# Weights of a 32-expert layer: 4 MB transfers in the second ring round and in the last expert but one

## What is computed

```python
logits = xf @ w_router + b_router
top_v, top_e = lax.top_k(logits, TOP_K)            # 4 of 32 experts a row
gates = jax.nn.softmax(top_v, axis=-1)
...
def run_block(args):                               # the rows of one expert
    e, toks, g = args
    xb = xf[toks]
    h = xb @ w1[e] + b1[e]                         # w1[e]: 1024 x 2048 float32, 8 MB
    glu = jnp.minimum(h[:, ::2], SWIGLU_LIMIT)
    lin = jnp.clip(h[:, 1::2], -SWIGLU_LIMIT, SWIGLU_LIMIT)
    a = glu * jax.nn.sigmoid(SWIGLU_ALPHA * glu) * (lin + 1)
    out = a @ w2[e] + b2[e]                        # w2[e]: 1024 x 1024 float32, 4 MB
    return out * g[:, None]
...
y = x2 + jax.nn.sigmoid(x2 @ w_ple_gate) * (p @ w_ple)
```

## Time and profile before

| | |
|---|---|
| median of 3 timed runs | 1106.73 us (1106.31 to 1110.37) |
| the profiled execution | 1111.12 us |
| its span, first to last instruction | 1109.3 us |
| TensorE busy | 1082.3 us, 98% of the span |
| VectorE, ScalarE, GpSimd busy | 40%, 14%, 7% |
| moved by transfers | 440.69 MB, 397 GB/s over the span |
| mean granted TensorE clock | 0.993 of full speed |

### The profile page before, as it was taken

The page is one execution under the profiler, slowest core; times in us unless marked ns, Lnnn a source line. Parts: engine busy times, 40 slices in busy tenths (PEclk is TensorE's granted clock), DMA queues, the critical chain, the costliest instruction groups (busy, mean ns, idle before and its releaser), DMA issues.

```text
span 1109.3 us, 14786 instructions
## 1 busy us (share of the span) xinstructions
PE 1082.3 (98%) x5608; PEld 426.0 (38%) x5608; DVE 438.5 (40%) x1109; ACT 159.6 (14%) x306; POOL 78.9 (7%) x107
## 2 busy tenths in 40 slices
PE   9999999999999999999999999999999999999998
PEld 7786423333333333333333333333333333333334
DVE  1648663333333333333333333333333333333345
ACT  1532331110000000000000000000000000000033
POOL 0747411000000000000000000000000000000000
PEclk9999979999999999999999999999999999999999
DMA  9989979999999999999999999999999999999961
GB/s 316 267 313 399 265 310 392 414 425 422 434 432 434 431 429 431 431 432 435 434 428 430 434 430 435 435 427 431 432 429 433 434 426 432 432 426 426 428 256 40
DMA packets 41027, 440.69 MB, mean 397 GB/s; under 512 B 8816, under 2 KB 16236, under 8 KB 25653
## 3 DMA queue, kind: packets, MB, share of 16 engines
q1 hardware_dynamic: 39945, 439.00, 95.0%
q0 software_dynamic: 368, 0.57, 0.3%
q10 hardware_dynamic: 676, 0.59, 0.2%
HBM read 436.61 MB, written 3.77 MB: 397 GB/s over the span
## 4 chain that ended last, share of the span: by engine, by line
PE 67%; DMA 20%; DVE 9%; issue 2%; POOL 1%; ACT 1%; DVEq 0%; SPq 0%; POOLq 0%; ACTq 0%
PE bank L1014 28%; DMA ring<-in_w_mlp 19%; PE bank L1092 16%; PE bank L961 5%; PE bank L605 3%; DVE proj L1651 3%; PE bank L1172 3%; PE bank L784 3%; DVE proj L1648 2%; DVE proj L1646 2%; PE bank L1073 1%; PE bank L974 1%; PE bank L1009 1%; POOL ring L2128 1%; PE bank L967 1%
## 5 line engine op out<-in xcount | busy, mean ns | idle before, releaser
L1014 PE MATMUL bank<-ring,proj 128*64 128x512 f32 x2024 | 463.2, 599 | 7.9 <-DMA ring<-in_w_mlp 7.9
L1612 DVE SCALAR_TENSOR_TENSOR xT<-bank,proj,xT 128x512 f32<-128x512 f32 x128 | 90.2, 746 | 431.2 <-PE bank L961 429.9
L1014 PEld LDWEIGHTS bank<-ring,proj 128*64 128x64 f32 x2024 | 137.7, 137 | 289.3 <-issue 263.6
L1092 PE MATMUL bank<-ring,pool_side 128*64 128x512 f32 x1024 | 226.8, 595 | 0.4 <-ACT pool_side L1981 0.4
L1092 PEld LDWEIGHTS bank<-ring,pool_side 128*64 128x64 f32 x1024 | 71.7, 137 | 133.3 <-issue 130.4
L1975 ACT ACTIVATE proj<-proj 128x256 f32<-128x256 f32 x64 | 26.7, 417 | 518.9 <-DVE proj L1645 518.9
L1603 DVE TENSOR_SCALAR proj<-bank,ln_rows_of_fours 128x64 f32<-128x64 f32 x256 | 67.4, 335 | 24.8 <-PE bank L974 24.8
L961 PE MATMUL bank<-mixT 64*128 64x512 f32 x264 | 74.5, 641 | 0.5 <-ACT mixT L1984 0.5
L605 PE MATMUL bank<-xT,ring 128*128 128x264 f32 x320 | 74.3, 388 | 0.3 <-ACT proj L1797 0.3
L605 PEld LDWEIGHTS bank<-xT,ring 128*128 128x128 f32 x320 | 60.0, 190 | 12.3 <-issue 1.6
L940 PE MATMUL bank<-xreg,proj 128*64 128x512 f32 x248 | 58.5, 592 | 0.0
(11 more groups left out here) (369 smaller groups left out, 638.5 us busy)
## 6 DMA issues: line engine op xcount, KB each, us to landing
ring<-in_w_mlp SPq DMA_DIRECT2D x77, 4096.0 KB, 27.2
ring<-in_w_mlp SPq DMA_DIRECT2D x36, 2048.0 KB, 12.1
ring<-in_w_in SPq DMA_DIRECT2D x9, 1024.0 KB, 15.2
ring<-in_w_out SPq DMA_DIRECT2D x4, 1024.0 KB, 9.0
ring<-in_w_ple_gate SPq DMA_DIRECT2D x4, 1024.0 KB, 28.5
xreg<-in_x_prompt SPq DMA_DIRECT2D x4, 512.0 KB, 4.1
ring<-q_row SPq DMA_DIRECT2D x1, 2048.0 KB, 7.3
ring<-k_row SPq DMA_DIRECT2D x1, 2048.0 KB, 7.2
```

The lines of the kernel that those rows point to most:

```text
L1014: last = pe.matmul(first_bank(t, q), xgT[:, k % 4, k // 4, :], first_columns(rows_, t, q), start=False, stop=(k == KD - 1))
L1092: last = pe.matmul(bank[4][BLOCK * h:BLOCK * (h + 1), :], aT[:, m, BLOCK * t:BLOCK * (t + 1)], w[:, k % 2, 512 * h:512 * h + 512], start=F ...
L1612: ins = STT(total[:, c, s], ins_bank[h][:, :], gate_table[:, c, bass.ds(n, 1)], total[:, c, s], ALU.mult, ALU.add)
```

## The change

The second and third ring round of the first body are loaded by a new function `load_quad` as eight transfers of 4 MB, each waiting for four used units, in place of sixteen of 2 MB, each waiting for two. In the last body only expert 31 is still loaded by pairs; expert 30 now comes as three 4 MB transfers in place of six pairs. `landed` follows: TensorE waits before every fourth unit there, and the counts that it waits for are adapted. `load_late(1)` stays behind the last transfer of the first body.

```diff
@@ -51,7 +51,7 @@
 SLOT = 2048
 UNITS = 12
 FIRST = 4
-LAST_PAIRS = (2, 3)
+LAST_PAIRS = (3,)
 COLUMNS_IN = (0, 512, 1024, 1536, 2048)
 T_U, T_Q, T_K, T_V, T_O = range(0, 20, 4)
 TILES = 20
@@ -447,6 +447,10 @@
                 sp.dma_start(pair_place(s), pair_weights(e, u)).then_inc(sem(f"slot{s}"), 16)
 
 
+            def load_quad(e, n):
+
+                sp.dma_start(quad_place(slot_of(n)), quad_weights(e, n % UNITS)).then_inc(sem(f"slot{slot_of(n)}"), 16)
+
             def load_next(n):
 
                 load_pair(n // UNITS, n // UNITS, n % UNITS)
@@ -487,10 +491,10 @@
             load_next(6)
             sp.wait_ge(sem("mix_ps"), 5)
             load_next(14)
-            for n in range(SLOTS, UNITS * STEP, 2):
-                sp.wait_ge(sem("units_used"), n - SLOTS + 2)
-                load_next(n)
-                if n == SLOTS + 30:
+            for n in range(SLOTS, UNITS * STEP, 4):
+                sp.wait_ge(sem("units_used"), n - SLOTS + 4)
+                load_quad(n // UNITS, n)
+                if n == SLOTS + 28:
                     sp.wait_ge(sem("ple_ps"), 3)
                     load_late(1)
 
@@ -508,7 +512,7 @@
                             load_pair(e + j, j, v)
                     else:
                         sp.wait_ge(sem("units_used"), done + (n - SLOTS + 4))
-                        sp.dma_start(quad_place(slot_of(n)), quad_weights(e + j, u)).then_inc(sem(f"slot{slot_of(n)}"), 16)
+                        load_quad(e + j, n)
 
             bodies = EXPERTS // STEP
             last = (bodies - 1) * STEP
@@ -977,12 +981,12 @@
             def landed(u, i4, closing, opening):
 
                 s = slot_of(u)
-                if opening:
+                if opening and u < SLOTS:
                     if u % 2 == 0:
                         pe.wait_ge(sem(f"slot{s}"), 16 * (before[s] + landings(u)))
                 elif closing == 2 and u // UNITS in LAST_PAIRS:
                     if u % 4 == 2:
-                        seen = STEP * UNITS // SLOTS + sum(slot_of(v) == s for v in range(UNITS * LAST_PAIRS[0], u + 1))
+                        seen = 1 + sum(slot_of(v) == s for v in range(UNITS * LAST_PAIRS[0], u + 1))
                         pe.wait_ge(sem(f"slot{s}"), 16 * (before[s] + seen))
                     elif u % 4 == 0:
                         pe.wait_ge(sem(f"slot{s}"), i4 * 12 + 16 * (before[s] + landings(u) - (s == slot_of(0))))
```

## The result

| | before | after |
|---|---|---|
| median of the timed runs | 1108.43 us (7 runs, 1106.31 to 1110.37) | 1112.93 us (7 runs, 1110.71 to 1115.61) |
| profiled execution, its span | 1111.12, 1109.3 us | 1114.90, 1113.1 us |
| mean granted TensorE clock of the profiled execution | 0.993 | 0.994 |

The ratio is 1.0043, with a 95% interval of 1.0027 to 1.0058: +4.5 us in the medians, +3.8 us between the two profiled spans. It is slower, by less than the 0.5% that counted as a difference. The forecast was +3.7 us.

The account below looks back on a forecast made before the run. The prediction took the weight queue, never resting from 244 us at 431 GB/s, to bound the kernel. Front +2.5 and expert 30 +1.2 gave +3.7 us on 1106.73, so 1110.4 us, range 1105.5 to 1115 us.

Parts of the forecast that it names:

- What bounds the kernel: From 244 us the weight queue runs at 431 GB/s without pause; time it loses earlier is lost at the end.
- The front step: Second ring round in 4 MB transfers: queue stays empty 5.7 us longer, first body transfer ends later, +2.5 us.
- The start-up: Second ring round: the empty queue begins, in effect, 1.4 us after its first issue, at 164.45.
- The bytes by 254 us: Queue from 157 to 254 us: 37.7 MB moved, before 38.7; more than 38.2 would refute the front step.
- The gaps: Among the eight 4 MB transfers: queue idle 1.1 us before the issue at 183.65, 0.9 before 213.74.
- The first wait: TensorE's first wait for weights comes one or two experts before 607 us.
- The lower bound of 0.9: Front step with no start-up at all: sixth issue still holds the end back to 255.1, at least +0.9 us.
- "hidden" rival: Front loss hidden: start-up next to nothing, no wait at expert 30; +0.9, 1107.6 us; chance 0.14.
- The end step: Expert 30: TensorE waits for whole 4 MB transfers, two waits of about half a microsecond; +1.2 us.
- Larger transfers save a fixed cost: Rival: each of eleven transfers fewer saves 2.2 us; -24 us, 1082 us; chance 0.06.
- 4 MB transfers flow worse beside the opening round's work: Rival: the eight transfers flow at 399 GB/s; +4.2 more, +7.9 in all, 1114.6 us; chance 0.16.
- The sum: Whole kernel: front 2.5 plus end 1.2 make +3.7 us, 1110.4 us, +0.33%; chance 0.64.

Follow-up runs that it names:

- e1: Changed kernel with 4 MB transfers in ring rounds two and three only, experts 30 and 31 in pairs: 1111.53 us, ratio 1.0027 to before.
- e3: Kernel before with the 2 MB transfers of rounds two and three issued by twos after four used units: 1111.58 us, ratio 1.0029 to before.
- e6: e1 with two 4 MB transfers issued together behind each wait for eight used units: 1120.99 us, ratio 1.0114 to before.
- e9: Kernel before with no pairs at the end, experts 30 and 31 both in 4 MB transfers: 1110.30 us, ratio 1.0025 to before.
- e2: Kernel before with only expert 30 in three 4 MB transfers, first body still in pairs: 1108.28 us, ratio 0.9998 to before.
- e5: Kernel before with all expert weights in 2 MB pairs, each behind a wait for two used units: 1112.96 us, ratio 1.0041 to before.
- e7: Kernel before with the first 4 MB transfer of the second body (expert 4) split into two pairs: 1108.28 us, ratio 0.9996 to before.

## Why the prediction was right

*What bounds the kernel* held: the steady rate stayed at 431 and 432 GB/s, waits for weights grew from 7.9 to 11.1 us, and a loss ahead of 244 us reached the end with nothing regained that the runs can show, in two sizes: 3.0 and 3.2 us where 2.5 was forecast (e1, e3), 12.6 where 12.2 was (e6).

*The front step*, +2.5 us: e1 measured 3.0 (1.4 to 4.5), and the trace of the change has 2.8, or 3.1 from its earlier issues. The start-up was as forecast: 374 x 7 = 2.62 MB by 170 us are 6.1 us at 431, so the queue began at 163.9, 1.2 us after its issue. The bytes by 254 us were forecast as 37.7 MB and were 37.5, so the first transfer of the body ended at 254 + (38.80 - 37.54) / 0.431 = 256.9 instead of the 256.5 forecast. The gaps are only in part where the forecast put them: against 431 GB/s the queue lost 1.1 us from 170 to 183 us (396), where none was forecast, 1.6 from 183 to 214 (409), where 1.1 was, and nothing from 214 to 244 (432), where 0.9 was. The 0.6 us that these 2.6 exceed the forecast 2.0 by are about what the term was too small; what slowed the queue from 170 to 183 us, at a transfer share of 1.00, is not shown. The first wait came two and a half experts earlier (75 us), not one or two: 2.8 us lost, at 1.28 us per expert, is already 2.2 experts, and I had not divided. The lower bound of 0.9 and the "hidden" rival are excluded by e1's and e3's intervals. That bound was no case of the model: it set an end without any start-up (255.1) against a measured one that contains it (254.2).

*The end step*, +1.2 us: 1.0 in the trace of the change (29.05 - 28.01), with waits of 0.48 and 0.27 where about half a microsecond each was forecast, and 1.0 and 1.2 for the two experts of e9's trace. As a time of its own it is not resolved (e2).

*The rivals.* "Larger transfers save a fixed cost" falls: e3 and e1 differ by nothing that can be measured. The fit in the Trainium skill, "DMA: Bandwidth & Descriptors", "Anatomy of one DMA — SWDGE (gpsimd) path", has about 2.0 us fixed for each transfer, for transfers that GpSimd issues. The trace of e5, with SyncE's transfers, does not agree for a queue that is kept full: the 326 MB of 756 us at 431 GB/s are 78 quads, and splitting them all cost 5.3 us of flow, 0.07 us for each. "4 MB transfers flow worse beside the opening round's work" falls as a price: 432 GB/s from 214 to 244 us, above the pairs' 427, and from 163.9 to 244 us, gaps included, 33.4 MB in 80.1 us, 417 GB/s, where the rival had 399 without gaps. From 170 to 183 us they did flow at 396, but the pairs had 363 there.

The sum, +3.7, lies within the measured interval (+3.0 to +6.4 us) and 0.1 us from the difference of the spans. So close a match is in part luck: the trace has 3.1 and 1.0, and the execution of the change reached the experts 0.4 us earlier. The absolute median came out 2.5 us above the forecast 1110.4, 1.7 of which is the median of before itself, which moved from 1106.73 in three runs to 1108.43 in seven.

## What to carry to other kernels

Before making transfers larger, ask what their wait becomes: a transfer of four slots waits for four, and when the queue is empty at that moment, the added wait is lost for good if the queue is the bound later. In this kernel small transfers paid where the queue waited for room and where the last experts waited for data, and large ones where the queue was never empty, where 4 MB instead of 2 MB gave 0.7% of flow. An engine that is busy 98% of the time can still be bound by a queue that is 5% slower (29.2 us for an expert against 27.9); look at who waits last, not at the busy share.

## What was not expected of the hardware

The scatter of the runs goes with TensorE's clock in one short stretch just ahead of the experts. In the profiled execution of before, the clock fell to its lower level (1.2 GHz) at 141 to 156 us (granted 0.54 of full speed over the stretch); in that of e3 it stayed at the upper one (2.4 GHz, granted 1.00). The windows of before and then of e3 (columns: length, busy time and count of TensorE matmul, its weight loads, VectorE, ScalarE, GpSimd, then granted clock, transfer share, GB/s):

```profile
135.00:141.00 6.00, 5.37 (x42) 2.58 (x40) 4.69 (x21) 3.35 (x8) 0.00 (x0) 1.00 0.90 356
141.00:156.00 15.00, 13.37 (x40) 4.38 (x42) 9.98 (x40) 5.51 (x9) 0.00 (x0) 0.54 0.73 311
```

```profile
135.00:141.00 6.00, 5.37 (x42) 2.82 (x40) 4.69 (x21) 3.66 (x8) 0.00 (x0) 1.00 0.86 326
141.00:156.00 15.00, 12.97 (x59) 4.55 (x60) 12.75 (x50) 5.21 (x9) 1.99 (x2) 1.00 0.75 320
```

TensorE did the same in both just ahead of the stretch: 5.37 us of 6, in 42 matmuls. At the full clock it then got through 59 matmuls where it got through 40 at the lower one, and since the first loads of round two wait for the first expert, the queue starts later too (the fourth unit is used at 163.05 in before, at 157.73 in e3): runs of before at a mean clock of 0.995 and below take 3.7 to 4.7 us longer. The same stretch goes with the clocks in between: from 135 to 165 us the profile of e5 (0.996) shows 0.89, those of before and e7 (0.993, 0.994) 0.77. Why it falls in one execution and not in the other these runs do not show. Runs of before at 0.999 and above lie within 1.7 us of each other in a group, all runs of a group within 8; comparing runs of equal clock is a finer measure than the medians.
